# Partition sums for norms: squares split into a rounded part and a rest, and two rounded matmul passes in place of one plain fp32 matmul

## The reference, cut to what matters

```python
def rmsnorm(x, g):
    y = xf * lax.rsqrt(jnp.mean(xf * xf, axis=-1, keepdims=True) + NORM_EPS)
    return (y * g.astype(jnp.float32)).astype(x.dtype)
...
    k = axial_rope(rmsnorm(k, k_g), row_ids, col_ids)            # first block, 2 key heads of 128
...
    ro = group_norm(ro, ret_norm)...                             # retention, 4 heads of 128
    dq = rms_norm(dq.reshape(shp_d), diff_q_norm)                # differential, 4 heads x 2 of 64
    dk = rms_norm(dk.reshape(shp_d), diff_k_norm)
    do = (rms_norm(do, diff_norm) * (1.0 - lam_init))...         # differential, 4 heads of 128
...
    k = rms_norm(kv[:, :, 0], k_norm)                            # memory keys, 4 heads of 256
```

## Time and profile before

| | |
|---|---|
| timed runs, us | 2104.71, 2106.89, 2106.92 (median 2106.89) |
| span of the profiled execution, us | 2101.4 |
| PE busy | 2056.6 us, 98% of the span |
| DVE busy | 1120.6 us, 53% |
| ACT busy | 891.7 us, 42% |
| POOL busy | 333.3 us, 16% |
| chain that ended last | PE 92%, DVE 4%, ACT 1%, SP's queue 1%, DMA 1% |

### The profile page before, as it was taken

The page is one execution under the profiler, slowest core; times in us unless marked ns, Lnnn a source line. Parts: engine busy times, 40 slices in busy tenths (PEclk is TensorE's granted clock), DMA queues, the critical chain, the costliest instruction groups (busy, mean ns, idle before and its releaser), DMA issues.

```text
span 2101.4 us, 25530 instructions
## 1 busy us (share of the span) xinstructions
PE 2056.6 (98%) x9996; PEld 1724.9 (82%) x9996; DVE 1120.6 (53%) x1988; ACT 891.7 (42%) x1755; POOL 333.3 (16%) x320
## 2 busy tenths in 40 slices
PE   8599999999999999999999999999999999999997
PEld 6598888888888888878888888788898888888886
DVE  5346778445544443476443435687775664444434
ACT  4224556234532332464332324677664443322324
POOL 3000533022000000332110101221211011110102
PEclk9699999999999999999999999999999999999999
DMA  7312111224332333233233223223152132332322
GB/s 161 59 51 67 55 51 51 75 86 153 108 100 95 96 100 95 76 110 100 91 100 101 92 89 111 85 66 106 61 175 91 36 105 91 101 100 92 100 90 71
DMA packets 61697, 191.45 MB, mean 91 GB/s; under 512 B 6884, under 2 KB 14564, under 8 KB 61576
## 3 DMA queue, kind: packets, MB, share of 16 engines
q1 hardware_dynamic: 61576, 189.82, 30.0%
HBM read 186.64 MB, written 2.10 MB: 90 GB/s over the span
## 4 chain that ended last, share of the span: by engine, by line
PE 92%; DVE 4%; ACT 1%; SPq 1%; DMA 1%; issue 0%; DVEq 0%; ACTq 0%
PE bank L292 91%; PE bank L297 1%; SPq L169 1%; DVE wl L469 1%; DVE tmp L181 1%; DMA bias<-tab_sb 0%; DVE work L190 0%; ACT wh L467 0%; DVE tmp L184 0%; DMA raw<-d_wts 0%; ACT rsq L178 0%; DVE x_sb L181 0%; DVE work L181 0%; DVE pd L184 0%; DVE pd L196 0%
## 5 line engine op out<-in xcount | busy, mean ns | idle before, releaser
L467 ACT ACTIVATE wh<-raw 128x512 fp32r<-128x512 f32 (+1 forms) x700 | 403.6, 609 | 915.8 <-PE bank L292 912.0
L292 PE MATMUL bank<-h_h,wh 128*128 128x512 f32 x1488 | 591.0, 397 | 7.2 <-ACT wh L467 6.2
L292 PE MATMUL bank<-h_l,wh 128*128 128x512 f32 x1488 | 581.9, 391 | 0.7 <-DVE h_l L184 0.7
L292 PE MATMUL bank<-h_h,wl 128*128 128x512 f32 x1488 | 581.4, 391 | 0.0
L469 DVE TENSOR_TENSOR wl<-raw,wh 128x512 fp32r<-128x512 f32 (+1 forms) x642 | 429.8, 694 | 61.7 <-ACT wh L467 39.8
L292 PEld LDWEIGHTS bank<-h_h,wh 128*128 128x128 f32 x1488 | 280.7, 189 | 68.5 <-ACT wh L467 6.2
L292 PEld LDWEIGHTS bank<-h_l,wh 128*128 128x128 f32 x1488 | 280.8, 189 | 60.6 <-DVE h_l L184 3.0
L292 PEld LDWEIGHTS bank<-h_h,wl 128*128 128x128 f32 x1488 | 280.5, 189 | 59.3 <-DVE wl L469 0.3
L469 POOL TENSOR_TENSOR wl<-raw,wh 128x256 fp32r<-128x256 f32 x114 | 94.6, 858 | 367.2 <-ACT wh L467 367.2
L202 POOL TENSOR_TENSOR tmp<-tmp,rstd 128x512 f32<-128x512 f32 x44 | 63.4, 1442 | 469.4 <-ACT tmp L178 469.4
L181 DVE TENSOR_TENSOR tmp<-bank,rstd 128x512 f32<-128x512 f32 x92 | 64.7, 706 | 116.7 <-PE bank L292 116.1
(11 more groups left out here) (473 smaller groups left out, 3513.1 us busy)
## 6 DMA issues: line engine op xcount, KB each, us to landing
raw<-d_wts SPq DMA_DIRECT2D x314, 512.0 KB, 3.5
raw<-d_wts SPq DMA_DIRECT2D x24, 384.0 KB, 3.0
x_sb<-d_xT SPq DMA_DIRECT2D x16, 256.0 KB, 5.4
raw<-d_wts SPq DMA_DIRECT2D x24, 128.0 KB, 2.0
d_yT<-x_sb SPq DMA_DIRECT2D x4, 384.0 KB, 2.9
tab<-d_ali SPq DMA_DIRECT2D x4, 256.0 KB, 4.0
tab<-d_dec SPq DMA_DIRECT2D x4, 256.0 KB, 3.6
mraw<-d_memT SPq DMA_DIRECT2D x8, 128.0 KB, 2.3
```

Of the source, the lines that this page charges most:

```text
L292: bank.done = pe.add(lambda e: e.matmul(out, lhsT, rhs, start=first, stop=True, skip_group_check=True), n, w, waits)
L467: p.th = [Op(act, lambda e, c=c: e.activation(H[:, c], raw[:, c], FN.Copy), [p.load]) for c in (slice(o, min(o + 512, width)) for o in ran ...
```

## The change: what it does

All plain fp32 sums of head norms over 256 or 512 columns go the way of `Sum.mean`. `halved` makes the rounded part on ACT and the rest on DVE, in the pair `rsqr0`, `rsqr1`; `rsq_mean` takes the pair first, splits, makes the two rounded passes, and lets `rsq` use the same pair as scratch. It is used by the two keys of the first block (`fin_k`), the eight differential queries and keys (`proj_d`) and the eight heads' outputs (`head_norm`). The memory keys' sums, two 256 wide tiles for each of four heads, are split into the halves of the same pair. The matrices for all of this are made by one wider copy at the start (128x512 in place of 128x128), over the place of the old ones.

The pair was taken after the matmul before, inside `rsq`. It is now taken before the split, and held until `rsq` is done.

```diff
--- before.py
+++ after.py
@@ -309,8 +309,10 @@
     cols_t = at("cols_sb", [128, NCOLS], O_K + 2.75)
     work_t = at("work", [128, 640], O_K + 3.5)
     ident = mats_t[:, 512:640]
-    mat = {n: mats_t[:, 128 * i:128 * i + 128] for i, n in enumerate(MATS)}
-    mat_r = at("m1024r", [128, 128], O_K, F32R)[:, :]
+    means_t = at("means", [128, 512], O_K, F32R)
+    mean = {n: means_t[:, 128 * i:128 * i + 128] for i, n in enumerate(MATS[:4])}
+    mat = {n: m.bitcast(F32) for n, m in mean.items()}
+    mat_r = mean["m1024"]
     eps_c, lnh_c = mats_t[:, 640:641], mats_t[:, 641:642]
 
     def col(name, k=0):
@@ -664,6 +666,25 @@
             u.free = [d2]
         return d1, d2
 
+    def halved(u, w, src, tok, n, lo=0):
+
+        h, l = (a[:, lo:lo + n] for a in u.parts)
+        th = a_act(h, src, FN.Copy, tok, w)
+        yield [th]
+        return (h, th), (l, v_tt(l, src, h.bitcast(F32), ALU.subtract, th, tok, w))
+
+    def rsq_mean(s, tok, m, n=S):
+
+        u, w = yield from grab(U)
+        parts = yield from halved(u, w, s, tok, n)
+        b = yield from bank_of(JOB)
+        for a, t in parts:
+            yield [t]
+            b_mm(b, b.ap[:, 0:n], m, a, t, t_mat_r)
+        d1, d2 = yield from rsq(b.ap[:, 0:n], s, n, b.done, tmp=[a[:, 0:n] for a in u.ap])
+        b.free, u.free = [d1], [d2]
+        return d2
+
     def a_square(out, src, *waits, **kw):
         return a_act(out, src, FN.Square, *waits, **kw)
 
@@ -836,7 +857,7 @@
 
     def first_mat():
         yield [t_mats]
-        t_mat_r.append(a_act(mat_r, mat["m1024"], FN.Copy, t_mats))
+        t_mat_r.append(a_act(means_t[:, :], mats_t[:, 0:512], FN.Copy, t_mats))
     first_load()
 
     h1 = Tiles("h1", O_A, KT)
@@ -1192,10 +1213,7 @@
 
     def fin_k(t, tc, tu, u, s, tsq, dst):
         yield [tsq]
-        b = yield from bank_of(JOB)
-        m = b_mm(b, b.ap[:, :], mat["m128"], s.ap[:, :], tsq, t_mats)
-        d1, d2 = yield from rsq(b.ap[:, :], s.ap[:, :], S, m)
-        b.free = [d1]
+        d2 = yield from rsq_mean(s.ap[:, :], tsq, mean["m128"])
         yield [tc, tu]
         td = e_tt(t.ap[:, :], t.ap[:, :], u.ap[:, :], ALU.add, tc, tu)
         u.free = [td]
...
@@ -1687,10 +1705,7 @@
         ts = a_act(s.ap[:, :], b.ap[:, :], FN.Square, b.done, w2)
         b.free = [ts]
         yield [ts]
-        b = yield from bank_of(JOB)
-        m = b_mm(b, b.ap[:, :], mat["m128"], s.ap[:, :], ts, t_mats)
-        d1, d2 = yield from rsq(b.ap[:, :], s.ap[:, :], S, m)
-        b.free = [d1]
+        d2 = yield from rsq_mean(s.ap[:, :], ts, mean["m128"])
         yield [d2]
         tk = v_stt(t.ap[:, :], t.ap[:, :], gcol, s.ap[:, :], ALU.mult, ALU.mult, tc, d2, tok)
         s.free = [tk]
...
@@ -1786,10 +1801,7 @@
             yield [tk]
             ts = a_act(s.ap[:, :], t.ap[:, :], FN.Square, tk, w2)
             yield [ts]
-            b2 = yield from bank_of(JOB)
-            m = b_mm(b2, b2.ap[:, :], mat["m64"], s.ap[:, :], ts, t_mats)
-            d1, d2 = yield from rsq(b2.ap[:, :], s.ap[:, :], S, m)
-            b2.free = [d1]
+            d2 = yield from rsq_mean(s.ap[:, :], ts, mean["m64"])
             if key == "dk":
                 tk = v_stt(t.ap[:, :], t.ap[:, :], dgain, s.ap[:, :], ALU.mult, ALU.mult, tk, d2, t_dg)
             else:
@@ -1926,13 +1938,18 @@
                 return
             ts = [keys_m[j, 0], keys_m[j, 1]]
             yield [ts[1][3]]
+            u, w = yield from grab(U)
+            parts = []
+            for n, (t, tk, s, tq) in enumerate(ts):
+                parts.extend((yield from halved(u, w, s.ap[:, 0:MEM], tq, MEM, MEM * n)))
             b = yield from bank_of(JOB)
-            for t, tk, s, tq in ts:
-                b_mm(b, b.ap[:, 0:MEM], mat["m256"], s.ap[:, 0:MEM], tq, t_mats)
+            for a, tk in parts:
+                yield [tk]
+                b_mm(b, b.ap[:, 0:MEM], mean["m256"], a, tk, t_mat_r)
             s0, s1 = ts[0][2], ts[1][2]
-            s1.free = [b.done]
-            d1, d2 = yield from rsq(b.ap[:, 0:MEM], s0.ap[:, 0:MEM], MEM, b.done)
-            b.free = [d1]
+            s1.free = [parts[3][1]]
+            d1, d2 = yield from rsq(b.ap[:, 0:MEM], s0.ap[:, 0:MEM], MEM, b.done, parts[1][1], tmp=[a[:, 0:MEM] for a in u.ap])
+            b.free, u.free = [d1], [d2]
             for n, (t, tk, s, tq) in enumerate(ts):
                 tk = v_stt(t.ap[:, 0:MEM], t.ap[:, 0:MEM], mgain[:, n:n + 1], s0.ap[:, 0:MEM], ALU.mult, ALU.mult, tk, d2, t_mg)
                 yield [tk]
...
```

More of the change, by code:

```diff
@@ L1211, in go @@
             for n in range(4):
-                m = b_mm(b, b.ap[:, n:n + 1], s.ap[:, 128 * n:128 * n + 128], mat["m128"][:, 0:1], tsq, t_mats)
+                m = b_mm(b, b.ap[:, n:n + 1], s.ap[:, 128 * n:128 * n + 128], mat["m128"][:, 0:1], tsq, t_mat_r)
             s.free = [m]
@@ L1767, in lambdas @@
         b = yield from bank_of(JOB)
-        m = b_mm(b, b.ap[:, 0:2], mat["m128"], lprod, t_lp, t_mats)
+        m = b_mm(b, b.ap[:, 0:2], mat["m128"], lprod, t_lp, t_mat_r)
         yield [m]
@@ L2069, in then @@
                 for s, ts in sq:
-                    m = b_mm(b, b.ap[:, n:n + 1], s.ap[:, 128 * n:128 * n + 128], mat["m256"][:, 0:1], ts, t_mats)
+                    m = b_mm(b, b.ap[:, n:n + 1], s.ap[:, 128 * n:128 * n + 128], mat["m256"][:, 0:1], ts, t_mat_r)
             for s, ts in sq:
```

## The result

The changed kernel takes 2138.8 us (four runs, 2137.4 to 2140.0) where the kernel before takes 2106.0 (four runs, 2104.7 to 2106.9): a ratio of 1.0158, 95% interval 1.0143 to 1.0172. That is 33 us slower. The prediction had the sign, the long wait and its length, but 2120.7 us, 18 too low, and the time lies above its range of 2107 to 2130.

What follows compares the result with a forecast made beforehand. PE's own work was taken to bound the kernel. -8.9 + 14.5 + 4.4 + 2.4 + 2.2 + 0.2, then -2 and +1, made +13.8 on a 2101.4 span; with 5.5 to the median, 2120.7 us, range 2107 to 2130.

Steps and rivals of the forecast that it cites:

- the long wait: End of `early`: PE stands while norms queue for the scratch pair and FIL banks are full; 15.8 us, costing 14.5.
- PE work saved: Rounded passes replace plain fp32 sums: 18 times 0.40 and 4 times 0.39 us on PE, together -8.9.
- `str1l`: Ahead of the end of `early`: PE waits for DVE's last `str1l` piece, behind a weight's DMA; 4.4 us, bounds 0 and 5.
- The memory tokens' tiles: Where `early` begins: their rests stand between weight pieces on DVE, so PE waits; 2.4 us, bounds 0 and 4.
- The clock: After the long wait PE runs 4.6 us of dense work at half clock, losing 2.2 us; bounds 0 and 7.
- Small waits: PE's own small waits in the stretch around 1500 to 1550 us mostly vanish behind the new wait: -2 us.
- The first block: The first block's attention, its order reshuffled too, gets some small waits back: +1 us.
- the one on what is added: Some 14 us on ACT and 16 on DVE of copies and subtractions cost nothing where PE has other fills.
- the long wait alone: Rival: the two smaller waits ahead of the end of `early` are hidden; +7 us, 2114, chance 0.20.
- Gain after all: Rival: no long wait at the end of `early`, only savings and small waits remain; 2099 us, chance 0.08.
- takes back just the saving: Rival: the wait cancels the saving, with no clock loss; within 0.2%, 2107 us, chance 0.05.
- Port and clock: Rival: POOL pieces delay the new subtractions (3.3 us) and the clock flickers after the stall (+5); 2129 us, chance 0.12.

Runs made afterwards that it cites:

- the two key norms alone: The changed kernel with only the two key norms of the first block (fin_k) split, all other means plain fp32: 2109.4 us, ratio 1.0023 to the kernel before.
- The price experiment: The kernel before, every instruction, with only the builder's price of a plain mean halved so it orders anew; some work moved to POOL: 2125.7 us, ratio 1.0097.
- the one pass in the old order: The kernel before in its own order, with squares written rounded and means as one rounded pass, no split, no hold: 2095.9 us, ratio 0.9955.

## Why the prediction was wrong

By its steps, in us of the profiled execution, forecast and measured (a wait is measured here as the time from one pass to the next, less what is usual for its shape):

- PE work saved, 8.9: borne out as far as rows show it; where nothing holds them up, `rsqr, means` passes take 0.23 as fills do.
- The long wait, 14.5: 14.6 (4.79, 0.50, 5.03, 0.55 and 3.76). Each of its legs was right to about 0.3. The last one I had added up too short: its terms give 3.2 without handovers, so 15.8 should have been 15.9 to 16.1, and 16.2 was measured.
- `str1l`, 4.4: 4.6 (the terms that I listed for it make 6.3 and not 6.0). The memory tokens' tiles, 2.4: 3.0.
- The clock, 2.2: 6.9. Windows of 2 us below full clock, each as busy time times what is missing of 1, give 1.7 at 1518 to 1522, after the wait for the memory tokens' tiles, where I had charged none, and 5.1 from 1538 to 1564. I charged only the dense passes after the wait and not the passes between the waits, which are slow too. That 4.6 us of dense passes came near was luck: I had read it from 91.8 to 96.4 us of the kernel before, but there PE had run without a gap since 81.8, on passes of 64 rows.
- Small waits, -2: about +5.5. Over the mixer, starts that come over 0.35 late sum to 27.5, against 3.5 before (late starts behind a plain sum, which are its own time, left out); without the three waits above 5.3 are left. The starts less late than that sum to 3.7 more.
- The first block, +1: +4.1, besides 3.4 of half clock. 3.1 of it are waits that I had not looked for: from 100 to 620 us PE waits 3.7 us in place of 0.6, mostly for `pta_l` and `outa_l` on DVE, and the kernel with the two key norms alone has the same ones.

These come to 33.2 of the 35.9 us between the spans; 2.7 I can't place. The clock was mis-sized, 2.2 for 6.9, and reached the upper bound that I had given it. The step that failed is the one on what is added: "over stages in which both have idle time, and where PE has other fills it costs nothing", and with it the lump of -2 and +1 for everything that I had not traced. I had read three places of the new order closely and taken the rest of it to be as good as the old. The runs show in its place about 5.5 us of small waits in the mixer where I had -2, and 4.1 in the first block where I had +1. The price experiment shows that a new plan needn't be as good as the old: 20 us for a plan alone. It does not show that 20 of the change's 33 are order, since each kernel has an order of its own; how the loss divides between the order and the added steps is open.

The half clock at 200 to 208 us must be told apart. The windows of the kernel before and of the changed one:

```profile
200.00:204.00 4.00, 4.00 (x27) 3.56 (x27) 3.93 (x10) 3.83 (x19) 0.00 (x0) 1.00 0.00 0
```
```profile
200.00:204.00 4.00, 4.00 (x19) 3.50 (x19) 3.93 (x9) 3.83 (x19) 0.00 (x0) 0.61 0.00 0
204.00:208.00 4.00, 4.00 (x16) 3.52 (x16) 2.07 (x4) 4.00 (x16) 0.00 (x0) 0.53 0.00 0
```

Of the fifteen later profiles thirteen show it, at a cost of 1.7 to 3.4 us each, that of the one pass in the old order too; the kernel before has none of it, but a low clock (0.83 over 40 to 60 us) ahead of its first long wait, where it costs nothing: that wait is 21.6 us long and ends at 81.8, and in the changed kernel, without the low clock, 24.7 and 81.9. Ahead of the dip, from 196.3 us on, PE runs the dilated bands' passes, 64 rows high, without a gap; the low clock of the kernel before at 41.8 stands behind such passes too, but those at 196 us go by without one there. It comes and goes, so I count only 4.1 of the 7.5 us lost in the first block as the change's. Nor does 5.5 us lie around the span, as I took it: in the changed kernel's runs it is 1.9, and the profiled execution of before, 2101.4 + 1.9, was 2.7 faster than the median. Against the span the forecast was 22 too low and not 18; that the half clock sets such executions apart fits in size and isn't shown.

The rivals: "the long wait alone" had the two smaller waits hidden, and both came, 4.6 and 3.0. "Gain after all" asked for less than 9 us at the long wait, and "takes back just the saving" for no clock loss. "Port and clock" came nearest in time, 2129, still 10 too low, and was half right: its clock, 7.2 with mine, is about the 6.9 measured, but the port added nothing to the long wait. Between 1542 and 1558 POOL does nothing, and the subtractions there take 0.68 and 0.42. Elsewhere it shows, in DVE's subtractions into `rsqr`:

```profile
L181 DVE TENSOR_TENSOR rsqr<-tmp,rsqr x18: 678/685/1054, 214.4 to 1547.4; 128x512 fp32r<-128x512 f32 x18
L181 DVE TENSOR_TENSOR rsqr<-ssum,rsqr x9: 418/693/1229, 22.5 to 1767.7; 128x512 fp32r<-128x512 f32 x8, 128x256 fp32r<-128x256 f32 x1
L181 DVE TENSOR_TENSOR rsqr<-mraw,rsqr x8: 411/424/1004, 1560.5 to 1593.4; 128x256 fp32r<-128x256 f32 x8
```

Six of these 35 take more than 0.8 us, up to 1.23, and each of the six began while POOL was already at a piece of its own; of the other 29, none above 0.7, 28 have no POOL instruction beside them, and one, at 1441.5, had begun before the POOL piece, which then took 1.09. DVE, then POOL:

```profile
214.41 1.05 DVE L181 TENSOR_TENSOR rsqr<-tmp,rsqr 128x512 fp32r<-128x512 f32 x1 [3.76 <-ACT rsqr L178]
```
```profile
213.48 2.58 POOL L471 TENSOR_TENSOR wl<-raw,wh 128x256 fp32r<-128x256 f32 x3 [21.14 <-ACT wh L469]
```

With the rule in the Trainium skill, "SBUF — State Buffer", section "Who interferes with whom", this trace agrees. It is rare: of the 26 subtractions that the change adds four are late, by 1.9 us together, and none of them in the long wait.

## What to carry to other kernels

Where a builder orders the instructions by its own prices, a change has two costs: its instructions and the new order. Try the second by itself, by changing a price and nothing else, before judging the first; in the one such order tried here it was worth 20 us of 2105, more than any saving on offer. A scratch tile that is taken one step earlier queues all who need it; look for the last one in that line and for what it alone can release. And of two ways to save PE time choose the one that adds no step between two engines: the single rounded pass in the old order, which leaves out the rests of the squares, gained 9.5 us, the exact split, whole or in part, lost in all ten forms in which it ran.

## What the runs showed of the hardware

In the changed kernel PE's granted clock fell to 0.50 (1.2 GHz) in and after waits of 2 to 5 us, and came back up to 5 us after PE was dense again (fills from 1558.0, full clock from about 1563). With 16 passes of 512 columns in each of the four long waits it stayed at 2.4 GHz there, and the mixer was 2.9 us shorter with 14.5 us more PE work in it. The half clock near 202 us came with PE busy without a gap, behind the same 64 row passes behind which other profiles, of the kernel before and of the one with the waits filled, had none; what brings it is open. A DVE subtraction with two inputs in SBUF took up to 1.23 us in place of 0.69 where it began during a POOL piece.
